# Routing in two halves round the middle of a unit, queries one head ahead in four blocks, scores at the fifth group

## The reference, cut to what matters

```python
q = (hf @ w_q).astype(jnp.float32).reshape(T, Hh, 2, PEER_QUERY_DIM // 2)
s1 = jnp.einsum('thd,nd->thn', q[:, :, 0], keys1.astype(jnp.float32))
s2 = jnp.einsum('thd,nd->thn', q[:, :, 1], keys2.astype(jnp.float32))
v1, i1 = lax.top_k(s1, K)
v2, i2 = lax.top_k(s2, K)
cand = (v1[..., :, None] + v2[..., None, :]).reshape(T, Hh, K * K)
sc, ci = lax.top_k(cand, K)
experts = (jnp.take_along_axis(i1, ci // K, axis=-1) * PEER_N_KEYS
           + jnp.take_along_axis(i2, ci % K, axis=-1))
wts = jax.nn.softmax(sc, axis=-1)
...
act = jax.nn.gelu(jnp.einsum('td,thkd->thk', h_c, u[e_c]).astype(jnp.float32))
return jnp.einsum('thk,thkd->td', (w_c * act).astype(v.dtype), v[e_c])
```

## Time and profile before

| what | value |
|---|---|
| median of 3 runs | 1257.22 us (1256.98 to 1259.14) |
| profiled execution, own time | 1255.68 us |
| its span, first to last instruction | 1253.9 us |
| PE busy | 1107.0 us (88%) |
| DVE busy | 702.7 us (56%) |
| POOL busy | 613.3 us (49%) |
| ACT busy | 522.1 us (42%) |
| DMA, read from HBM | 353.65 MB |

### The profile page before, as it was taken

One profiled execution on the slowest core, in us unless ns is written; L12 is line 12 of the kernel. 1 busy time (PEld: TensorE's weight loads), 2 busy tenths in 40 slices (PEclk: granted clock), 3 DMA queues, 4 the chain that ended last, 5 costly groups with the idle time before them and its releaser, 6 DMA issues.

```text
span 1253.9 us, 17339 instructions
## 1 busy us (share of the span) xinstructions
PE 1107.0 (88%) x5405; PEld 762.4 (61%) x5405; DVE 702.7 (56%) x1691; ACT 522.1 (42%) x1036; POOL 613.3 (49%) x448
## 2 busy tenths in 40 slices
PE   8989999999999999999878797797887978877776
PEld 5869999999998999985434253253432524322222
DVE  4535555554542333225766766676666776677554
ACT  4555556565566777512332233322333232321211
POOL 2376776567664766742234334343353433443431
PEclk9999999999999999999999999999999999999999
DMA  7353232233333433865799999999999999999996
GB/s 259 119 168 115 93 128 100 100 117 100 118 102 117 135 135 115 320 259 218 294 422 397 422 411 413 422 407 423 422 414 422 418 422 422 411 422 422 422 421 284
DMA packets 61014, 355.23 MB, mean 283 GB/s; under 512 B 7983, under 2 KB 8494, under 8 KB 27054
## 3 DMA queue, kind: packets, MB, share of 16 engines
q0 software_dynamic: 36864, 268.45, 52.0%
q1 hardware_dynamic: 24110, 86.27, 19.8%
HBM read 353.65 MB, written 1.05 MB: 283 GB/s over the span
## 4 chain that ended last, share of the span: by engine, by line
PE 56%; DMA 28%; issue 7%; ACT 3%; DVE 3%; POOL 3%; DVEq 0%; POOLq 0%; ACTq 0%; SPq 0%
DMA top<-peer_uv_dram,route 24%; PE ps L1821 12%; PE ps L1472 8%; PE ps L1473 8%; PE ps L1474 8%; PE ps L1784 4%; DMA front<-peer_uv_dram,route 2%; PE ps L1769 2%; PE ps L1632 2%; POOL split L932 2%; PE ps L1651 2%; PE ps L1650 2%; DMA front<-branch_tiles_dram 1%; ACT top L877 1%; ACT split L563 1%
## 5 line engine op out<-in xcount | busy, mean ns | idle before, releaser
L932 POOL TENSOR_TENSOR split<-front,split 128x1024 fp32r<-128x1024 f32 x123 | 297.6, 2432 | 174.1 <-ACT split L563 173.7
L1821 PE MATMUL ps<-top 128*128 128x512 f32 x640 | 301.2, 610 | 90.3 <-ACT top L877 90.2
L982 POOL DMA_INDIRECT top<-peer_uv_dram,route x160 | 165.4, 1034 | 255.2 <-PE ps L1821 246.2
L1821 PEld LDWEIGHTS ps<-top 128*128 128x128 f32 x640 | 116.7, 192 | 261.3 <-ACT top L877 150.5
L1331 DVE CUSTOM_DVE_ANT_0 top<-top,scratch 128x1024 f32<-128x1024 f32 x160 | 196.0, 1225 | 141.6 <-DMA top<-peer_uv_dram,route 141.6
L1472 PE MATMUL ps<-split 128*128 128x256 f32 (+1 forms) x768 | 241.2, 314 | 6.6 <-POOL split L932 3.4
L1473 PE MATMUL ps<-split 128*128 128x256 f32 (+1 forms) x768 | 224.3, 292 | 0.0
L1474 PE MATMUL ps<-split 128*128 128x256 f32 (+1 forms) x768 | 224.3, 292 | 0.0
L877 ACT ACTIVATE top<-cst,route 128x128 f32<-128x128 f32 x256 | 88.8, 394 | 273.1 <-DVE route L1339 270.6
L563 ACT ACTIVATE split<-front 128x1024 fp32r<-128x1024 f32 x128 | 133.4, 1057 | 135.0 <-PE ps L1474 108.4
L1472 PEld LDWEIGHTS ps<-split 128*128 128x128 f32 x768 | 147.0, 191 | 13.7 <-issue 8.5
(11 more groups left out here) (266 smaller groups left out, 1600.0 us busy)
## 6 DMA issues: line engine op xcount, KB each, us to landing
front<-in_tiles_dram SPq DMA_DIRECT2D x80, 512.0 KB, 3.3
front<-branch_tiles_dram SPq DMA_DIRECT2D x24, 512.0 KB, 4.2
front<-in_w_in_dram SPq DMA_DIRECT2D x8, 512.0 KB, 4.3
front<-in_w_mem_kv_dram SPq DMA_DIRECT2D x8, 512.0 KB, 3.7
front<-kv_tiles_dram SPq DMA_DIRECT2D x8, 512.0 KB, 3.7
top<-in_w_out_dram SPq DMA_DIRECT2D x8, 512.0 KB, 6.1
rest<-peer_w_q_by_head_dram SPq DMA_DIRECT2D x3, 1024.0 KB, 8.9
gate_part<-peer_w_q_by_head_dram SPq DMA_DIRECT2D x3, 1024.0 KB, 16.2
```

What stands on the lines that cost most here:

```text
L932: pool.tensor_tensor(halves[i % 3][:, 1], raw[i % 3], halves[i % 3][:, 0], ALU.subtract).then_inc(lo_ready, 1)
L982: pool.indirect_dma_start(rows_uv[k % RING], None, peer_uv, bass.IndirectOffsetOnAxis(ap=idx[c][:, k:k + 1], axis=0)).then_inc(s_row[k % R ...
L1821: ins = pe.matmul(ps[:, 2 * c + half, :], diag[:, k % 8, :], rows_uv[k % RING][:, D + half * 512:D + (half + 1) * 512], start=False, stop= ...
```

## The change

**DVE.** `route_steps` becomes two generators: `route_keys` (5 steps: the best 16 of both key lists and the 256 sums) and `route_experts` (9 steps: the rest, up to `idx`). In unit n the experts' half for unit n + 1 goes behind dots 0 to 8, and the keys' half for unit n + 2 behind dots 11 to 15. `weigh` goes from k = 7 to k = 10. The whole routing of unit 1 ahead of the first dot goes away; unit 0 carries all 14 steps of it, two behind each dot.

**PE.** The queries of head 1 ahead of the loop go away. In the loop the queries are those of head h + 1, and each half i is split in two blocks of 8 records, so four blocks, before groups 0 to 3 of the first unit of head h; the scores come before group 4 of it. In `first_head` the transposes of the second half of `x1` come after the first 8 query records and not after 16.

**ACT.** Copies of queries and scores follow (after groups 1, 3 and 4 of the first unit), the moves of weights go to the second unit, and the exponentials for unit n + 1 go before group 3 of unit n.

```diff
-            def body_act(h, project, route_next, j=None, par=None):
+            def body_act(h, j=None, par=None, project=True, last=False):
+                n = h * NC
                 for g in range(NG):
-                    if g == NG - 1 and route_next:
-                        exps_act(h * NC + 2)
-                    group_act(h * NC, 0, g)
-                    if project:
+                    if g == 3:
+                        exps_act(n + 1)
+                    group_act(n, 0, g)
+                    if project and g in (1, 3):
+                        keep_q(h + 1, g // 2)
+                    if project and g == 4:
+                        keep_scores(h + 1)
+                for g in range(NG):
+                    if g == 3 and not last:
+                        exps_act(n + 2)
+                    group_act(n + 1, 1, g)
+                    if j is not None:
                         move_wq(h, j, par, g)
...
-                    if k == 7 and not first and not last:
-                        weigh(n + 1, other if c else par, 1 - c)
...
-                    if k >= 3 and steps is not None:
-                        next(steps, None)
-                if steps is not None:
-                    next(steps, None)
+                    if k < 9 and experts is not None:
+                        next(experts, None)
+                        if first:
+                            next(experts, None)
+                    if k == 10 and not last:
+                        weigh(n + 1, other if c else par, 1 - c)
+                    if k >= 11 and keys is not None:
+                        next(keys, None)
...
             weigh(0, 1, 0)
-            whole_route(1, 1)
-            weigh(1, 1, 1)
...
                 for half in range(2):
-                    if half:
-                        turn_x1(c, 1)
                     pe.wait_ge(d_turned, 2 * c + half + 1)
                     for i in range(2):
                         ins = query(0, i, c * P, (c + 1) * P, range(4 * half, 4 * half + 4))
+                        if half == 0 and i == 0:
+                            turn_x1(c, 1)
...
                 for g in range(NG):
+                    if not last and g == 0:
+                        pe.wait_ge(wq_moved, moved)
+                    if not last and g < 4:
+                        ins = query(1 - par, g // 2, 0, T, range(4 * (g % 2), 4 * (g % 2) + 4))
+                        if g % 2:
+                            ins.then_inc(done("p_q"), 1)
+                    if not last and g == 4:
+                        head_scores(h + 1)
                     rows_pe(h * NC, 0, g, last)
                 for g in range(NG):
-                    if project is not None and g == 1:
-                        pe.wait_ge(wq_moved, project)
-                    if project is not None and g in (1, 2):
-                        query(par, g - 1, 0, T).then_inc(done("p_q"), 1)
-                    if project is not None and g == 3:
-                        head_scores(h + 2)
                     rows_pe(h * NC + 1, 1, g, last)
...
-            pe.wait_ge(s_wq[1], 16)
-            for i in range(2):
-                head_query(1, i)
-            head_scores(1)
```

More of the change, by code:

```diff
@@ L1 @@
+import itertools
 from contextlib import ExitStack
@@ L343, in hybrid_layer @@
         zero = words(0, P + 512)
-        RSTEPS = 13
+        RSTEPS, KEY_STEPS = 13, 5
         FILLS = (8, 3, 2, 3, 2)
@@ L885, in move_wq @@
                                wq_later[par][:, bass.ds(j * (KT * QW) + g * piece, piece)], ACT.Copy).then_inc(wq_moved, 1)
-            def body_act(h, project, route_next, j=None, par=None):
+            def body_act(h, j=None, par=None, project=True, last=False):
+                n = h * NC
                 for g in range(NG):
-                    if g == NG - 1 and route_next:
-                        exps_act(h * NC + 2)
-                    group_act(h * NC, 0, g)
-                    if project:
-                        move_wq(h, j, par, g)
[L895 to L902, removed]
+                    if g == 3:
[10 more added lines that the diff above has]
+                    if j is not None:
+                        move_wq(h, j, par, g)
             def norm_act(c):
@@ L915, in _ @@
             first_head(1)
[L916 to L919, removed]
+            act.wait_ge(s_wq[1], 16)
+            act.sem_inc(wq_moved, NG)
             act.wait_ge(s_wq_later, 16 * (PHEADS - 2))
@@ L922, in _ @@
                 for par in range(2):
-                    body_act(j * 2 + par, True, True, j, par)
-            body_act(PHEADS - 2, False, True)
-            body_act(PHEADS - 1, False, False)
+                    body_act(j * 2 + par, j, par)
+            body_act(PHEADS - 2)
+            body_act(PHEADS - 1, project=False, last=True)
         @block.gpsimd
@@ L1256, in _, with route_links @@
                     dve.tensor_tensor(mixT[:, 2 * m:2 * m + 2, :], mixT[:, 2 * m:2 * m + 2, :], prod[i % 2], ALU.add).then_inc(done("br_sum"), 1)
-            def route_steps(n, c, scores):
-                step = [0]
+            def route_links(n, first_step):
+                step = [first_step]
                 def link(ins):
@@ L1285, in best, with route_keys @@
                     linked()
+                return link, linked, best
+            def route_keys(n, c, scores):
+                link, linked, best = route_links(n, 0)
                 dve.wait_ge(done("p_sk"), scores)
@@ L1294, in route_steps, with route_experts @@
                 yield
+            def route_experts(n, c):
+                link, linked, best = route_links(n, KEY_STEPS)
                 linked()
@@ L1317, in route_steps @@
                                          op0=ALU.mult, op1=ALU.add).then_inc(done("idx_ready"), 1)
-                assert step[0] == RSTEPS
             def weigh(n, par, c):
@@ L1345, in add_out, with unit_dve @@
                                   ALU.add).then_inc(p_end, 1)
-            def unit_dve(n, c, par, steps, first=False, last=False):
+            def unit_dve(n, c, par, experts, keys, first=False, last=False):
                 other = par * -1 + 1
@@ L1356, in unit_dve @@
                         coefficients(n, c, k // GROUP - 1, par)
-                    if k == 7 and not first and not last:
-                        weigh(n + 1, other if c else par, 1 - c)
                     if k == 12 and last:
                         add_out(0)
-                    if k >= 3 and steps is not None:
-                        next(steps, None)
-                if steps is not None:
-                    next(steps, None)
-            def body_dve(h, par, route_next, first=False):
-                unit_dve(h * NC, 0, par, route_steps(h * NC + 2, 0, score_count(h + 1)) if route_next else None, first)
-                unit_dve(h * NC + 1, 1, par, route_steps(h * NC + 3, 1, score_count(h + 1)) if route_next else None,
-                         last=not route_next)
+                    if k < 9 and experts is not None:
[6 more added lines that the diff above has]
+                        next(keys, None)
+            def body_dve(h, par, route_next, first=False):
+                n = h * NC
+                experts = itertools.chain(route_keys(1, 1, 2), route_experts(1, 1)) if first else route_experts(n + 1, 1)
+                unit_dve(n, 0, par, experts, route_keys(n + 2, 0, score_count(h + 1)) if route_next else None, first)
+                unit_dve(n + 1, 1, par, route_experts(n + 2, 0) if route_next else None,
+                         route_keys(n + 3, 1, score_count(h + 1)) if route_next else None, last=not route_next)
             def add_x1(c, n):
@@ L1395, in whole_route @@
             def whole_route(n, c):
-                for _ in route_steps(n, c, n + 1):
-                    pass
+                for half in (route_keys(n, c, n + 1), route_experts(n, c)):
+                    for _ in half:
+                        pass
             dve.wait_ge(s_x1, 16 * NC)
@@ L1806, in first_head @@
                 scores(c).then_inc(done("p_s"), 1)
-            def head_query(h, i):
-                query(h % 2, i, 0, T).then_inc(done("p_q"), 1)
             def head_scores(h):
@@ L1823, in rows_pe, with body_pe @@
                     ins.then_inc(done("vrow"), 1)
-            def body_pe(h, par, project, last=False):
+            def body_pe(h, par, moved, last=False):
                 for g in range(NG):
+                    if not last and g == 0:
[6 more added lines that the diff above has]
+                        head_scores(h + 1)
                     rows_pe(h * NC, 0, g, last)
                 for g in range(NG):
-                    if project is not None and g == 1:
-                        pe.wait_ge(wq_moved, project)
-                    if project is not None and g in (1, 2):
-                        query(par, g - 1, 0, T).then_inc(done("p_q"), 1)
-                    if project is not None and g == 3:
```

(3 more changed lines are left out.)

## The result

The changed kernel takes 1243.15 us in the median of 4 runs (1239.78 to 1243.96) against 1257.3 of before; the ratio is 0.988 with a 95% interval of 0.986 to 0.990. The forecast was 1242.8. Measured again later it took 1242.24 us (6 runs), ratio again 0.988 (0.986 to 0.990).

A forecast was written before the change was run, and what follows sets the result against it. The prediction took the DMA transfers (422 GB/s) as the bound. Its terms, 0.8 + 9.6 - 1.0 + 5.0 = 14.4 us, off 1257.22 gave 1242.8 us; range 1239.5 to 1248.5 for 8 in 10, forecast 62%.

The forecast's parts named there:

- Term 1: First head: transposes after 8 query records let the first gather leave 0.8 us earlier, between 0 and 1.0.
- Term 2: Unit 0: the transfers' shortage from 608 to 628 closes as first dots come earlier; 9.6 us less 1.0 for thin margin.
- Term 4: Query units: five rate drops vanish with queries in four blocks and later scores; 5.0 us, bounds 0 and 5.9.
- The doubt from the DMA share near 1.00 in the dips: Busy DMA near 1.00 in four rate drops, less well explained by starving; so 5.0 us taken, not 5.9.
- Terms at 0: Unit 1's later index list, DVE's added wait, moved weights and exponentials before group 3 were each to cost 0.
- both rivals: Shortage moves within unit 0 and rate drops in query units stay as well: 1251 us; both partly, 5%.
- The hole didn't move: Rival: in unit 0, buffers return too slowly, 5 us idle between 612 and 630; 1246.8 us, chance 14%.
- the dips didn't stay: Rival: query units' rate drops have another cause than PE's lateness, such as issue bursts or memory; 1247.8 us, chance 15%.
- The wait at k = 11: DVE waits for copied scores before dots of rows 12 on; hidden with 2.5 us, some 3 us in unit 0.
- its fifth step: Added waits on DVE, moves of weights and exponentials before group 3: cost 0, though DVE may be held in unit 0.
- One of its signs: In query units, no idle time of POOL over 3 us before a gather, with 420 GB/s there.
- the slower rival: DVE's wait at k = 11 becomes pacemaker, with PE at half clock in two groups a head; 1271 us, chance 4%.

The follow-up runs named there:

- the blocks alone: Kernel before with only the queries in four blocks before groups 0 to 3, scores before group 4, copies moved to match: 1253.83 us, ratio 0.996.
- The halves before groups 1 and 2: Changed kernel with each query half whole (16 records) before groups 1 and 2 of a head's first unit, not four blocks: 1252.61 us, ratio 0.996.
- the two kernels told above: Changed kernel with unit 1's whole routing on DVE before the first dot: 1254.14 us; changed kernel with head 1's queries and scores before the first rows: 1251.42 us.

## Why the prediction was right

**What bounds it** held: the transfers. Windows of 20 us of the changed kernel read 420 to 422 GB/s from 610 to 1210.

**Term 1** (transposes), 0.8 predicted: 0.78 by both executions and 0.79 by its undoing.

**Term 2** (the hole), 8.6 net: the same 40 us from the first gather read 295 GB/s before and 396 after, 40 x 101 / 422 = 9.6 us. The 1.0 us that I took off for the thin margin wasn't needed. The steps came out as worked: less the 2.47 us by which the part ahead was longer, the first dot began at 594.30 (near 594.3 predicted) and the first gather left at 585.59 (585.6). The ninth gather left 18.1 us after the first (18.0 predicted, 603.6 - 585.6), DVE waited 1.53 us at k = 11 in unit 0 (up to 3), and unit 1's `idx` came at 613.50 without anyone waiting. What the prediction lacked is a second cause. It named DVE's routing as what kept the first dot. ACT's first gelu was kept just as long by the copies of head 1's scores; in the kernel before it ends at 610.98, and the third dot, behind which DVE takes the first coefficients, at 611.02:

```profile
609.49 1.28 ACT L873 ACT_TABLE_LOAD   x1
610.78 0.20 ACT L873 ACTIVATE route<-route 128x2 f32<-128x2 f32 x1
...
610.94 0.08 DVE L1331 DVE_READ_ACCUMULATOR2_ANT route<- 128x1 f32 x1
611.09 0.16 DVE L1339 TENSOR_TENSOR route<-route 128x2 f32<-128x2 f32 x1
```

Undoing either alone loses 11.3 or 8.4 us. The two don't add up: the first product goes by the later of them. The change removes both, so the sum came out; with one of them alone nearly the whole term would have been predicted and not gained.

**Term 4** (the dips), 5.0: the rest of the gather stage, 13.87 - 9.6 = 4.3 us, and 4.1 by the blocks alone. The length of PE's blocks is the cause: short ones take the dips out of the kernel before, and long ones bring them back in the changed one, in neither case with a change of routing (ACT's copies moved along with the blocks). The doubt from the DMA share near 1.00 in the dips was unfounded. The ring's "4 to 4.7 us" of slack, for which the prediction shows no working, was if anything too high: two halves make PE 3.8 us late by its own count, and the dips are there.

**Terms at 0** (later `idx`, new waits, moved weights, moved exponentials) held in the changed order. The halves before groups 1 and 2 show that the last one depends on where ACT's copies stand.

**How close it came** is partly luck. The hole gave 1.0 us more than its term and the dips 0.7 less, which nearly cancel, and the forecast lies 0.4 us from a median of four runs that spread over 4.2 us. One sum is slightly off: with both rivals, 14.4 - 4 - 5 = 5.4 us are left and the time is 1251.8, not 1251.

**The rivals.** The hole didn't move and the dips didn't stay. The wait at k = 11 occurs once, in unit 0, where the prediction allows for it in its fifth step, though its list of what would be wrong names such a wait without that exception. One of its signs wasn't met to the letter: POOL waited 3.37 us ahead of the gather at 868.73, in a query unit, but the rate stayed at 422 GB/s from 850 to 870 and 421 from 870 to 890. Half clock, the condition of the slower rival, did appear: in the two kernels told above, after waits of PE of 9.63 and 3.15 us, and in the changed kernel itself, where after a wait of 2.25 us the granted clock from 727 to 735 was 0.79. There the rate stayed at 422 GB/s, so it cost nothing. The Trainium skill's rule on the SBUF interfaces that POOL shares with VectorE (GPSIMD Engine Reference, Specifications) changed nothing in the sum. The changed kernel's issues took 0.94 us in the median and up to 1.99, and its transfers kept their rate. No run shows what makes an issue slow; the small dip of the version with late transposes stands beside three slow ones.

## What to carry to other kernels

Where a ring of buffers feeds saturated transfers, cut the work beside it into blocks of about the spare time of one period. Here blocks of 1.72 us, with 1.54 to spare, cost nothing that could be measured, and blocks twice as long cost 5.3 us of the gather stage, or 8.5 where they also held up ACT. Before moving what holds a first result, list everything queued ahead of each engine's share of it, ACT's copies and table loads too: the result waits for the latest of them, and removing one of two gained next to nothing here. When runs differ by more than the edit is worth, measure it as a distance between two instructions inside one trace, and see first how much that distance differs between two executions of the same kernel.

## What the runs showed of the hardware

The part ahead of the change, the same program in all kernels, ended between 567.03 and 573.52 (addition of `x1`'s second half) in twelve profiled executions. It goes roughly by PE's mean granted clock in the first 50 us. At 1.00 it ended at 567.03 and 567.18, at 0.97 between 568.89 and 571.64, at 0.93 between 571.35 and 572.26, at 0.90 at 573.52. That is 6.5 us, 0.5% of the span, and nearly half of what the change gives. The two go together in these executions; that the clock is the cause isn't shown. Why the clock comes up later in one execution than in another stays open.

In three places PE's granted clock was below 1.00 in or right behind a wait of PE: 0.50 from 606 to 616 with a wait of 9.63 us, 0.56 from 612.50 to 616.00 behind one of 3.15 us, 0.79 from 727 to 735 behind one of 2.25 us. Four records of the row's product took 3.78 us in the first and 3.47 us in the second, where they take 1.88 to 1.99 at a granted clock of 1.00.
